# Experts in order of their count, and gate and up weights in long rows, in a hybrid attention, convolution and expert layer

## What is computed

```
h2 = modulate(rms_norm(x, norm2_g), sh2, sc2)              # (2048, 1024)
g_idx = argmax(h2 @ w_rg + b_rg)                           # group of a token
top_v, top_i = top_k((h2 @ w_re + b_re)[group g_idx], 2)   # two experts in it
gates = softmax(top_v) * p_group
y[tok] += gate * ((silu(xb @ w_gate[e]) * (xb @ w_up[e])) @ w_down[e])   # for each expert e, its tokens xb
x = x + g2 * y ;  out = rms_norm(x, final_g)
```

## Time and profile before

| | us |
|---|---|
| median of three runs | 2000.89 (1994.81 to 2002.94) |
| span of the profiled execution | 1996.9 |
| busy in it: TensorE matmul, weight load | 1804.3, 1482.5 |
| VectorE, ScalarE, GpSimd | 1181.1, 854.9, 855.0 |

### The profile page before, as it was taken

The page is one execution under the profiler, slowest core; times in us unless marked ns, Lnnn a source line. Parts: engine busy times, 40 slices in busy tenths (PEclk is TensorE's granted clock), DMA queues, the critical chain, the costliest instruction groups (busy, mean ns, idle before and its releaser), DMA issues. The chain is left out here.

```text
span 1996.9 us, 26921 instructions
## 1 busy us (share of the span) xinstructions
PE 1804.3 (90%) x8987; PEld 1482.5 (74%) x8988; DVE 1181.1 (59%) x2015; ACT 854.9 (43%) x1520; POOL 855.0 (43%) x887
## 2 busy tenths in 40 slices
PE   2999999997999999999995999965999999999970
PEld 2777878764777777777784788854999988888960
DVE  4687889956766766666645555553444444444434
ACT  3535454326777677667684132311222222222214
POOL 0132314103888888888892111122243434434330
PEclk9999999996999999999996999977999999999995
DMA  7656555530000000000006344415899998999948
GB/s 282 197 164 185 172 163 165 147 95 0 6 9 6 9 9 6 11 7 6 11 11 218 105 157 141 143 43 189 278 268 276 279 276 270 278 276 274 272 91 336
DMA packets 216176, 291.05 MB, mean 146 GB/s; under 512 B 24373, under 2 KB 172048, under 8 KB 215834
## 3 DMA queue, kind: packets, MB, share of 16 engines
q1 hardware_dynamic: 193498, 220.60, 33.3%
q0 software_dynamic: 20224, 69.22, 13.9%
q10 hardware_dynamic: 2368, 0.17, 0.1%
HBM read 229.13 MB, written 60.82 MB: 145 GB/s over the span
## 5 line engine op out<-in xcount | busy, mean ns | idle before, releaser
L1212 POOL TENSOR_TENSOR plo<-KR,phi 128x512 fp32r<-128x512 f32 (+1 forms) x320 | 352.3, 1118 | 44.8 <-ACT KR L1171 44.6
L1020 DVE TENSOR_REDUCE cmax<-tbank 128x1 f32<-128x512 f32 (+2 forms) x320 | 193.4, 605 | 106.4 <-PE tbank L835 101.2
L1170 ACT ACTIVATE phi<-tbank 128x512 fp32r<-128x512 f32 (+1 forms) x320 | 170.7, 533 | 141.6 <-PE tbank L884 137.1
L387 PE MATMUL pbank<-hhi,wslhi 128*128 128x512 f32 x512 | 207.9, 406 | 6.7 <-DVE wsllo L440 6.7
L1946 DVE TENSOR_SCALAR xTe<-ebank,modcol 128x256 f32<-128x256 f32 (+1 forms) x128 | 53.7, 472 | 258.9 <-PE ebank L1864 137.6
L387 PE MATMUL pbank<-hhi,wsllo 128*128 128x512 f32 x512 | 201.9, 394 | 0.0
L387 PE MATMUL pbank<-hlo,wslhi 128*128 128x512 f32 x512 | 201.9, 394 | 0.0
L331 POOL DMA_DIRECT2D wmod<-in_w_ada x64 | 48.4, 757 | 305.2 <-DVE macc L519 295.2
L1886 PE MATMUL ebank<-xTe,wg 128*128 128x192 f32 x1024 | 171.8, 326 | 3.1 <-DVE ahi L1974 1.8
L1886 PEld LDWEIGHTS ebank<-xTe,wg 128*128 128x128 f32 x1024 | 167.9, 190 | 7.9 <-DVE ahi L1974 2.1
L1886 PE MATMUL ebank<-xTe,wu 128*128 128x192 f32 x1024 | 171.6, 326 | 0.0
(11 more groups left out here) (283 smaller groups left out, 3976.8 us busy)
## 6 DMA issues: line engine op xcount, KB each, us to landing
wg<-in_w_exp_gate SPq DMA_DIRECT2D x32, 1024.0 KB, 5.9
wu<-in_w_exp_up SPq DMA_DIRECT2D x32, 1024.0 KB, 9.0
wd<-in_w_exp_down SPq DMA_DIRECT2D x32, 1024.0 KB, 7.6
wraw<-in_w_in SPq DMA_DIRECT2D x60, 512.0 KB, 4.2
wmod<-in_w_ada POOLq DMA_DIRECT2D x64, 256.0 KB, 3.4
xt<-in_x SPq DMA_DIRECT2D x4, 2048.0 KB, 12.7
wada<-in_w_ada SPq DMA_DIRECT2D x4, 2048.0 KB, 18.7
mixed<-mix_dram SPq DMA_DIRECT2D x16, 512.0 KB, 4.3
```

The source lines that it names most:

```text
L387: ins = pe.matmul(out, w[:, S % 3, k], h[:, n % 2, k], start=k == 0 and j == 0, stop=k == KD - 1 and j == 2)
L1020: W(ve.tensor_reduce(cmax[:, i % 2, n:n + 1], plain[:, chunk % 2, 0:w], AX.X, ALU.max), plain_read)
L1170: A(act.activation(step_of(phi, m), scores[:, m % 2, j * P:512], ACT.Exp), phi_done)
L1212: po.tensor_tensor(step_of(plo, m), step_of(probs, m), step_of(phi, m).bitcast(F32), ALU.subtract).then_inc(plo_done, 1)
```

## The change

Three parts.

1. *Order and second tiles.* `route` also sorts: a 32x32 comparison of the counts (64 times the count less the expert's number) gives each expert its place, and one matmul turns that into `order` (the expert at each place) and `isb` (1 for the first 20 places). `experts` walks the places. Places 0 to 19 (10 pairs, `PAIRS_B`) are as before. Places 20 to 31 have tile a alone: 128 columns in gate and up, no transposes of `xb`, no `down_rest`, no `yb`. If more than 20 experts have over 128 rows, `rounds` becomes at least 2. Each engine that addresses an expert's data reads its number from `order` into a register (`expert_at`).
2. *Weights in long rows.* `wg` and `wu` are loaded with rows 8p to 8p+7 on partition p, 8 KB at a time. Channels therefore stand as p*8+k: `modc`, the router's weights and biases (`own`) and xs are arranged in that order, xs by the VectorE operation that writes it.
3. Small things that follow: `slot_b` as two tables that are added, a hold on `down_a` in place of `down_b` where there is no second tile, rank lowered by 128 or 192 at the end of the tables.

```
-            wgd = T["w_exp_gate"].rearrange("l e (k p) n -> p (l e k) n", p=P)
+            wgd = T["w_exp_gate"].rearrange("l e (p k) n -> p (l e) (k n)", k=KD)
...
+                        e = expert_at(sp, r, ep, b)
                         sp.wait_ge(up_done, r * NEXP + ep * 2 + (b + 1))
-                        sp.dma_start(wg[:, b], wgd[:, bass.ds(ep * 2 * KD + b * KD, KD), :]).then_inc(ld_gu[b], 16)
+                        sp.dma_start(wg[:, b:b + 1].rearrange("p b k n -> p b (k n)"), wgd[:, bass.ds(e, 1), :]).then_inc(ld_gu[b], 16)
...
+        def expert_at(eng, r, q, b):
+            return eng.value_load(order[0:1, bass.ds(r * 0 + q * 2 + b, 1)], min_val=0, max_val=NEXP - 1)
+        def pairs(eng, body):
+            with eng.Fori(0, PAIRS_B - 1) as q:
+                body(q, True, True)
+            body(PAIRS_B - 1, True, False)
+            body(PAIRS_B, False, False)
+            with eng.Fori(0, PAIRS - 2 - PAIRS_B) as i:
+                body(i + PAIRS_B + 1, False, False)
...
+                def pair(q, rest, ahead):
+                    gate_up(q, 1, r, rest)
+                    turn_even(q + 1, r, (0, 1), ahead)
+                    down_first(q, 0, r, rest)
+                    turn_even(q + 1, r, (2, 3), ahead)
+                    if rest:
+                        down_rest(q, 0, r)
+                    gate_up(q + 1, 0, r, ahead)
+                    turn_odd(q + 1, r)
+                    down_first(q, 1, r, rest)
+                    if rest:
+                        down_rest(q, 1, r)
...
             def gate_up(q, b, r, rest):
+                n = CAP if rest else P
+                cols = cols_of[b] if rest else tile_cols[b]
...
-                            ins = pe.matmul(out[:, f * CAP:(f + 1) * CAP], w[:, b, k, f * P:(f + 1) * P],
-                                            xT[:, k, cols_of[b]], start=k == 0, stop=k == KD - 1)
+                            ins = pe.matmul(out[:, f * n:(f + 1) * n], w[:, b, k, f * P:(f + 1) * P],
+                                            xT[:, k, cols], start=k == 0, stop=k == KD - 1)
```

In `route`, before the rank arithmetic, and behind it:

```
+            few, iota, count = slice(0, NEXP), cst[0:NEXP, C_EXP:C_EXP + NEXP], bank[:, 1, 0:NEXP]
+            do(ve.scalar_tensor_tensor(key[:], count[few], 64.0, iota, ALU.mult, ALU.subtract))
+            do(ve.tensor_tensor(above[:], key[:], cst[few, C_ID:C_ID + NEXP], ALU.mult))
+            do(ve.tensor_reduce(place[:, 0:1], above[:], AX.X, ALU.add))
+            do(ve.tensor_scalar(above[:], key[:], place[:, 0:1], None, ALU.is_gt))
+            do(ve.tensor_reduce(place[:, 1:2], above[:], AX.X, ALU.add))
+            do(ve.tensor_scalar(place[:, 2:3], place[:, 1:2], float(NEXP_B), None, ALU.is_lt))
...
+            do(ve.tensor_scalar(large[:], count, float(P), None, ALU.is_gt))
+            do(ve.tensor_reduce(wide[:], large[:], AX.X, ALU.add))
+            do(ve.tensor_scalar(wide[:], wide[:], float(NEXP_B), 1.0, ALU.is_gt, ALU.add))
+            do(ve.tensor_tensor(need1[:], need1[:], wide[:], ALU.max))
             do(ve.tensor_copy(rounds[:], need1[:]))
+            ve.wait_ge(ordered, 1)
+            V(ve.tensor_copy(order[:], bank[:, 2, 0:NEXP]))
+            do(ve.tensor_copy(isb[:], bank[:, 2, NEXP:2 * NEXP]))
```

In `mix`:

```
-                    ins = pe.matmul(turn[:, 0, k:k + 1], macc[:, 2 + k // 4, k % 4 * P:(k % 4 + 1) * P],
+                    half = macc[:, 2 + k // KD * 2:4 + k // KD * 2].rearrange("p a n -> p (a n)")
+                    ins = pe.matmul(turn[:, 0, k:k + 1], half[:, k % KD::KD],
                                     cst[:, C_ONE:C_ONE + 1], start=True, stop=True)
...
-                ve.tensor_scalar(xs[:, b], x2[:, b], xstat[:, b, 2:3], None, ALU.mult).then_inc(xs_ready, 1)
+                ve.tensor_scalar(xs[:, b].rearrange("t (k p) -> t k p", k=KD), x2[:, b].rearrange("t (p k) -> t k p", k=KD),
+                                 xstat[:, b, 2:3], None, ALU.mult).then_inc(xs_ready, 1)
```

On GpSimd, with an A pair's part (`rest` false):

```
+            def scatter(q, b, r, rest):
+                e = expert_at(po, r, q, b)
                 hold(po, st_ya[b], r * (PAIRS * 16) + q * 16, passed_pool)
+                po.tensor_copy(ja[:, b:b + 1], dest_a[:, bass.ds(e, 1)]).then_inc(dest_copied, 1)
...
                 put(ya[:, b], ja[:, b:b + 1], st_ya[b])
+                if rest:
+                    hold(po, yb_done, r * NEXP_B + q * 2 + (b + 2), passed_pool)
+                    put(yb[:, b], jb[:, b:b + 1], st_yb[b])
```

More of the change, by code:

```diff
@@ L43 @@
 CAPB = CAP - P
+PAIRS = NEXP // 2
+PAIRS_B = 10
+NEXP_B = 2 * PAIRS_B
 ROUNDS = -(-S // CAP)
@@ L1527, in _ @@
             act.dma_start(rbias[:, NGRP:], T["b_router_expert"][0, :].partition_broadcast(P)).then_inc(ld_r, 16)
+            for j in range(2):
+                act.dma_start(own[:, j], T["b_ada"][0, (3 + j) * D:(4 + j) * D].rearrange("(p k) -> p k", k=KD)
+                              ).then_inc(ld_r, 16)
+            act.dma_start(own[:, 2], T["norm2_g"][0].rearrange("(p k) -> p k", k=KD)).then_inc(ld_r, 16)
             def mixers_in(t, b):
@@ L1587, in route @@
         sem = lambda name: ctx.enter_context(nc.semaphore(name))
-        cst, logits, gates, rank, marks, rounds = (st[k] for k in (
-            "cst", "logits", "gates", "rank", "marks", "rounds"))
+        cst, logits, gates, rank, marks, rounds, pick, order, isb = (st[k] for k in (
+            "cst", "logits", "gates", "rank", "marks", "rounds", "pick", "order", "isb"))
         g1, gexp, gcand, gone, gpen = (sb(n, [P, NT, NGRP]) for n in ("g1", "gexp", "gcand", "gone", "gpen"))
@@ L1719, in _ @@
             ins.then_inc(ranked, 1)
+            pe.wait_ge(places_ready, 1)
+            pe.matmul(bank[:, 2, 0:2 * NEXP], oneb[0:NEXP], sorter[:].rearrange("p a e -> p (a e)"), start=True, stop=True
+                      ).then_inc(ordered, 1)
 def experts(nc, T, st):
@@ L1837, in _ @@
-                with po.Fori(0, PAIRS - 2) as q:
-                    gather_even(q + 2, r)
-                    scatter(q, 0, r)
-                    gather_odd(q + 2, r)
-                    scatter(q, 1, r)
+                hold(po, dump_ready, 3, passed_pool)
+                hold(po, table_ready, r * 5 + 3, passed_pool)
+                for q in range(2):
+                    gather_even(q, r, True)
+                    gather_odd(q, r, True)
+                hold(po, table_ready, r * 5 + 5, passed_pool)
@@ new lines, in pair @@
+                def pair(q, rest, ahead):
+                    gather_even(q + 2, r, ahead)
+                    scatter(q, 0, r, rest)
+                    gather_odd(q + 2, r, ahead)
+                    scatter(q, 1, r, rest)
+                with po.Fori(0, PAIRS_B - 2) as q:
+                    pair(q, True, True)
+                for q in (PAIRS_B - 2, PAIRS_B - 1):
+                    pair(q, True, False)
+                with po.Fori(0, PAIRS - 2 - PAIRS_B) as i:
+                    pair(i + PAIRS_B, False, False)
@@ L1998, in _ @@
                              ).then_inc(dump_ready, 1)
+            for b in range(2):
+                ve.memset(slot_b[(1 - b) * CAPB:(2 - b) * CAPB, b], 0).then_inc(dump_ready, 1)
             with ve.Fori(0, n_rounds) as r:
@@ L2214, in program @@
         st["marks"], st["rounds"] = keep("marks", [P, NT, 2, MARKS * NEXP], BF16), keep("rounds", [P, 1], I32)
+        st["pick"] = keep("pick", [P, NT, 2, NEXP])
+        st["order"], st["isb"] = keep("order", [P, NEXP], I32), keep("isb", [P, NEXP])
         route(nc, T, st)
```

312 lines of the change are left out of this document (170 added, 142 removed).

## The result

The changed kernel takes **1948.46 us** (median of 4 runs, 1944.7 to 1950.75), the kernel before beside it 2001.85 us (4 runs, 1994.81 to 2002.94). The ratio is 0.9746, 95% interval 0.9723 to 0.977: faster by 2.5%. The prediction was 1941 us, 1927 to 1963. The profiled spans are 1996.9 and 1946.9 us, so the change takes 50.0 us where the sum said 59.7. All ratios here leave out one slow execution, of 3849.73 us, among the ten of the kernel before with a swap.

A forecast was written before the change was run, and what follows sets the result against it. TensorE was taken to bound the expert stage, DMA engines close behind. 78.7 us saved, less 5.5, 5, 3.5, 1, 2.5 and 1.5, gave 59.7, say 60: span 1996.9 to 1937, median 1941 us, range 1927 to 1963.

The forecast's parts named there:

- TensorE's share: Expert stage: twelve experts lose their second tile; shorter products, no second down product, fewer transposes save 78.7 us.
- Uncovered copies: Pairs without a second tile: the next product waits 1.1 us for copies, five pairs, -5.5 us (4 to 8).
- DMA engines full: Pairs without a second tile need about 23.8 us of DMA time, TensorE 22.5: -5 us, ends 0 and 15.
- Routing: Routing: fourteen small uncovered VectorE steps, 0.25 us each with their waits, cost 3.5 us.
- First loads: Start of expert stage: register reads delay first loads, weights pass faster; -1 us, ends -4 and +1.
- Tail: End of expert stage: only some 3 of the last 5.6 us taken from TensorE are won, -2.5 us.
- Mixing stage: New column order: xs write could double at no cost, modulation matmuls slow down; -1.5 us taken.
- Modulation matmuls: Mixing stage: sixteen matmuls take weights at a step of 8 floats; ends 0 and 6.7, -1.5 us taken.
- 1, the DMA engines take over: Expert stage: long rows may bring nothing, some 18 us of waiting instead of 5: 1954 us; chance 0.20.
- 2, nothing collides: No DMA wait in the expert stage, and start and modulation cost nothing: 1933 us; chance 0.10.
- 3, register reads on GpSimd: Pairs with second tiles: five reads each outgrow GpSimd's idle time; at 5 us a read 2057 us; chance 0.03.
- 4: More than 20 experts have over 128 tokens, so the whole expert stage runs twice: about 2440 us; chance 0.02.

The follow-up runs named there:

- the kernel before with a swap: Kernel before, with VectorE's next-tile mixing scale (mstat) moved ahead of the write of xs: 1996.59 us, ratio 0.9978.
- copies covered: In pairs without a second tile, even down product split around the second transposes, on the changed kernel with mixing scale first and small loads on GpSimd: 1937.51 us.

## Why the prediction came out as it did

The time was inside the range, and the gain 50 us by the profiles, 53 by the medians, for the 60 forecast. By its own steps:

- **TensorE's share** (78.7 us): right. A product saves 3.2 us rather than 3.36 (38.5 in all, not 40.3), the pace being the load's 0.113 and not the 0.110 between; 76.9 in all.
- **Uncovered copies** (-5.5): right, 1.13 us of waiting in each of five pairs. By the length of a pair, 22.97 against 21.57 us for the first with its copies covered, it is 1.4, 7.0 in all.
- **DMA engines full** (-5, ends 0 and 15): 0. Its own working, five pairs of 1.3 us less the lead of 3, gives 3.5 and not the 5 taken. An A pair was put at 24.8 us of share, 23.8 of time; the runs put it at 22.4, while TensorE with the uncovered copy wants 22.97. The view of the DMA queues for 1765 to 1853 us, in the kernel that stands at the limit (copies covered), splits it:

```profile
q1 hardware_dynamic: 4512, 25.36, 70.0%
q0 software_dynamic: 2122, 7.71, 33.0%
```

For a pair of 22.3 us that is 15.6 us for the weights, as the 15.8 forecast from the 4 KB rate, but 7.4 for GpSimd's gathers and puts, where 9.0 had been taken, most of it from two windows of 4 us in the tail. The size of that one piece turned a wait into none. That the two paces nearly meet, 22.4 and 22.97, is also why the cover is worth little. And here is the luck: these 5 us that were not lost stand against 1.8 won less in the products and 1.5 lost more in the copies, so that the stretch of pairs came out at its forecast.
- **Routing** (-3.5): 4.9, since three of fourteen steps took 0.58 to 0.75 us, and a register read is in it.
- **First loads** (1 us lost): 2.1 won. The weights pass faster: this part is 29.06 us before and 29.17 with the order alone, 26.92 with the rows alone and in the changed kernel, and the wait for xb fell from 9.30 to 7.70 us.
- **Tail** (-2.5): right. From expert 30's down product to the final loads 28.07 us became 25.08, 3.0 won of 5.6 as forecast.
- **Mixing stage** (-1.5): **this step failed**, at 12.5. The write of xs was costed at nothing because "its reader, eight transposes of the next step, comes 9 us later, and VectorE is not the bound". Both are true, and neither was the question. The one who waits for the write is not its reader but what is queued behind it: `mstat`, then ScalarE's copy, then TensorE. The 12 us named as the price if that cover went took a doubled write in 16 tiles; the write grew by 0.45 us and was paid in 13 steps, 5.7. And the three loads of `own` on ScalarE's queue, 3.6 us of issue ahead of the first copy, had no term at all.
- **Modulation matmuls** (0 to 6.7, taken at 1.5): 1.1 us by the two traces, and 0.7 for the clock that comes back later. This size came out by luck. The 6.66 us from which the ends were worked out were run mostly at the 1.2 GHz level, which the row doesn't show; the same matmuls take 4.12 us in the kernel with the order alone, and against that the step of 8 floats costs 3.6. The Trainium skill's page "SBUF — State Buffer", in its section on the DMA port swizzle, has a penalty for steps above 16 bytes. The trace bears it out: at full clock the step of 32 bytes takes TensorE's records here from some 0.11 to 0.24 us, and VectorE's scaling from 0.754 to 1.21. The prediction's reason for the lower end, that its rows "show no slower reading", was one of rows that read no such step.

**Rivals.** 1, the DMA engines take over: not in the changed kernel, but it is what happens with short rows. The Trainium skill, "DMA: Bandwidth & Descriptors", Specifications, has 512 B as the least length at line rate. In the windows from 1780 to 1849 us, 1 KB rows bring 341 to 352 GB/s, with TensorE waiting, and 8 KB rows 361 to 374, with TensorE setting the pace, and up to 376 at their limit. So the trace disagrees, and these 6% decide whether TensorE waits. 2, nothing collides: true of the expert stage, not of the mixing stage. 3, register reads on GpSimd: B pairs are 34.48 us, against 34.46 before, so no read is anywhere near 2.7 us; GpSimd stood 0.53 us between its copies of indices where one read lies. 4: one round, 32 loads of `wg`.

The order alone is worth -2.7%, the rows alone +0.5%, both -2.5%. The long rows cost 12.5 us in a stage that the change only touches in passing, and win about 11 back (1946.74 us for the order alone, against 1948.46 - 12.5) in six pairs and at the stage's start; once most of their cost is taken away they are a small gain: with the swap and the copies covered 1937.51 us (1936.88 to 1939.02) against 1942.02 for short rows (1940.02 to 1943.66).

## What to carry to other kernels

Ask of an operation that gets slower not only who reads its result but who stands behind it in its engine's queue, and follow that chain to the bounding engine: a product that starts "without a gap" may be one that two chains reach at the same moment, with no slack in either. Loads issued by a computing engine are work of that engine, above all ahead of its first operation in a stage. And a layout that makes transfers better is paid where the layout is produced; put the strided operation last in its queue. Before two durations on TensorE are compared, or one is taken as a price, read the granted clock of both.

## What the runs showed of the hardware

- A VectorE scaling of 128x1024 float32 that reads at a step of 8 floats takes 1.21 us against 0.754.
- TensorE records of one column whose weights are read at a step of 8 floats take some 0.24 us at the 2.4 as at the 1.2 GHz level (12 in a window of 2.70 us, 18 in 3.90). Without the step it is 0.11 and 0.21 (27 in 2.80 us, 27 in 5.50). Thirty-two of them took 7.74 us with the step in every trace, without it 4.12 to 6.66.
- With rows of 8 KB the DMA share of a window in A pairs stands at 1.02 to 1.03 at any rate from 344 to 390 GB/s, with and without waits for its transfers. So the share doesn't tell if one more byte makes a wait; the rate held over whole pairs, 376 GB/s here, does.
- A wait of 2 us on TensorE costs more than its length: the next 32 records took 5.46 us instead of 3.74, with the granted clock at 0.50 for some 3 us after it.
